# The first feed-forward's down projection as seven half-sized products

## What is computed

```python
def causal_dwconv(x, w, b):
    y = lax.conv_general_dilated(x, w[:, None, :], window_strides=(1,), padding=[(K - 1, 0)],
                                 feature_group_count=C)
    return y + b

def conv_ffn(h, w_up, conv_w, conv_b, w_down):
    a = causal_dwconv(h @ w_up, conv_w, conv_b)
    gate, val = jnp.split(a, 2, axis=-1)
    return (jax.nn.silu(gate) * val) @ w_down

x = x + conv_ffn(rms_norm(x, norm_ffn_g[l]), ffn_w_up[l], ffn_conv_w[l], ffn_conv_b[l], ffn_w_down[l])
```

## Time and profile before

| | before |
|---|---|
| median of 3 runs | 2004.89 us (2002.77 to 2004.93) |
| profiled execution, its own time | 2004.43 us |
| its span | 2002.7 us |
| TensorE busy | 1975.7 us |
| VectorE busy | 1243.9 us |
| ScalarE busy | 875.4 us |
| GpSimd busy | 109.8 us |
| first feed-forward, transposes of its norm to those of the next | 645.9 to 1010.3 us |
| second feed-forward, likewise | 1598 to 1933 us |

### The profile page before, as it was taken

One profiled execution on the slowest core, in us unless ns is written; L12 is line 12 of the kernel. 1 busy time (PEld: TensorE's weight loads), 2 busy tenths in 40 slices (PEclk: granted clock), 3 DMA queues, 4 the chain that ended last, 5 costly groups with the idle time before them and its releaser, 6 DMA issues.

```text
span 2002.7 us, 23836 instructions
## 1 busy us (share of the span) xinstructions
PE 1975.7 (99%) x9638; PEld 1629.4 (81%) x9638; DVE 1243.9 (62%) x1734; ACT 875.4 (44%) x1222; POOL 109.8 (5%) x120
## 2 busy tenths in 40 slices
PE   8999999999999999999999999999999999999998
PEld 7887788878888888888888688888888888888876
DVE  6857657577444766366468878743444476858676
ACT  5647633456323433133342634542323363544555
POOL 0004300221000000000010300000000000000000
PEclk9999999999999999999999999999999999999999
DMA  4320022222433333333342123232323335233122
GB/s 136 105 84 23 22 84 85 94 69 69 133 99 105 85 88 102 101 89 95 97 136 94 64 74 98 71 102 87 105 86 104 100 110 168 63 106 128 41 100 80
DMA packets 164444, 184.47 MB, mean 92 GB/s; under 512 B 6759, under 2 KB 125798, under 8 KB 164334
## 3 DMA queue, kind: packets, MB, share of 16 engines
q1 hardware_dynamic: 161006, 175.03, 27.4%
q10 hardware_dynamic: 2624, 5.78, 0.9%
q0 software_dynamic: 704, 2.13, 0.4%
HBM read 180.81 MB, written 2.12 MB: 91 GB/s over the span
## 4 chain that ended last, share of the span: by engine, by line
PE 93%; DVE 4%; ACT 2%; issue 1%; DMA 0%; POOL 0%; DVEq 0%; SPq 0%; ACTq 0%; POOLq 0%
PE ps L516 29%; PE ps L518 28%; PE ps L517 28%; PE ps L640 2%; PE ps L675 1%; PE ps L656 1%; PE ps L712 1%; PE ps L901 1%; ACT HH L1552 0%; DVE WL L2106 0%; DVE arena_r L2986 0%; DMA W<-in_w_in_dram 0%; DVE slots_r L2106 0%; DVE arena L2915 0%; ACT WH L1488 0%
## 5 line engine op out<-in xcount | busy, mean ns | idle before, releaser
L516 PE MATMUL ps<-HH,WH 128*128 128x512 f32 (+1 forms) x1464 | 559.3, 382 | 2.5 <-DVE HL L2234 2.5
L517 PE MATMUL ps<-HL,WH 128*128 128x512 f32 (+1 forms) x1464 | 556.3, 380 | 0.0
L2106 DVE TENSOR_TENSOR WL<-W,WH 128x2048 fp32r<-128x2048 f32 (+2 forms) x150 | 340.2, 2269 | 284.9 <-ACT WH L1488 284.2
L518 PE MATMUL ps<-HH,WL 128*128 128x512 f32 (+1 forms) x1336 | 506.6, 379 | 0.0
L1488 ACT ACTIVATE WH<-W 128x2048 fp32r<-128x2048 f32 (+2 forms) x151 | 284.2, 1884 | 190.2 <-DMA W<-in_ffn_w_down_dram 46.5
L516 PEld LDWEIGHTS ps<-HH,WH 128*128 128x128 f32 x1464 | 275.6, 188 | 56.5 <-issue 2.6
L517 PEld LDWEIGHTS ps<-HL,WH 128*128 128x128 f32 x1464 | 275.6, 188 | 51.6 <-issue 0.2
L518 PEld LDWEIGHTS ps<-HH,WL 128*128 128x128 f32 x1336 | 251.4, 188 | 47.6
L516 PE MATMUL ps<-WH,arena_r 128*128 128x512 f32 (+1 forms) x584 | 227.1, 389 | 2.3 <-DVE slots_r L2106 1.7
L518 PE MATMUL ps<-WH,arena_r 128*128 128x512 f32 (+1 forms) x584 | 226.5, 388 | 0.0
L517 PE MATMUL ps<-WL,arena_r 128*128 128x512 f32 (+1 forms) x456 | 176.7, 387 | 0.0
(11 more groups left out here) (400 smaller groups left out, 2607.2 us busy)
## 6 DMA issues: line engine op xcount, KB each, us to landing
W<-in_w_in_dram SPq DMA_DIRECT2D x50, 1024.0 KB, 5.2
W<-in_ffn_w_up_dram SPq DMA_DIRECT2D x44, 512.0 KB, 5.1
arena<-in_w_ff_dram SPq DMA_DIRECT2D x18, 1024.0 KB, 5.3
W<-in_w_gate_dram SPq DMA_DIRECT2D x16, 1024.0 KB, 4.9
W<-in_w_ff_dram SPq DMA_DIRECT2D x14, 1024.0 KB, 5.2
W<-in_ffn_w_down_dram SPq DMA_DIRECT2D x10, 1024.0 KB, 5.0
W<-in_w_out_dram SPq DMA_DIRECT2D x8, 1024.0 KB, 5.0
W<-in_w_branch_dram SPq DMA_DIRECT2D x8, 1024.0 KB, 5.1
```

Of the source, the lines that this page charges most:

```text
L516: pe.matmul(out_, st[0], mv[0], start=first, stop=False, skip_group_check=chained)
L517: pe.matmul(out_, st[0], mv[1], start=False, stop=False, skip_group_check=chained)
L518: return pe.matmul(out_, st[1], mv[0], start=False, stop=last, skip_group_check=chained)
L2106: dve.tensor_tensor(low[:, 0:n], raw[:, 0:n], plain(WH[:, j % RING, 0:n]), ALU.subtract).then_inc(slab_lo, 1)
```

## The change

The four stages become one, `ffn1`. The 11 pairs of hidden tiles are taken in chunks of 2, 3, 3 and 3. TensorE makes the up tiles of a chunk and, but for the last chunk, the first tile of the next one, then the seven products of the chunk, each of pairs x 2 x 3 matmuls. A new class `Seven` holds the semaphores and the chunk sizes. The blocks of down weights are loaded into the arena, four DMAs a chunk; the part slabs need no load of their own. t1, t3, t4 are made in the arena (t1 in b12's place, t4 in b21's), t2 in a slot of `W`. The low parts lie in `WL` or in the arena. Taps stay on VectorE. A tile's taps, gate product and forms now stand together in VectorE's queue, where they were one or two tiles apart. The first and the last line of the SP part show when the next up slabs are loaded.

```diff
+            def pe_ffn1():
+                done = 0
+                for c in range(len(F1.pairs)):
+                    for i in range(done, min(FT, 2 * F1.before(c + 1) + 1)):
...
+                        if i == 0:
+                            gemm_f_by_halves(("up", i), w, 2)
+                            ring[:] = [6, 7, 2, 3]
...
+                    down_parts(c)
+            def down_parts(c):
...
+                        elif ks[0] == 0:
+                            pe.wait_ge(F1.chain_read, 8 * c + {"P6": 0, "P3": 2, "P7": 4, "P4": 6}[name] + t + 1)
...
+                products(0, part_slab(0), range(pairs))
+                m = 1
+                if last:
+                    ws = [part_slab(1), part_slab(2)]
+                    for ks in (range(pairs - 1), range(pairs - 1, pairs)):
+                        for j in range(2):
+                            products(1 + j, ws[j], ks)
+                    m = 3
+                for m in range(m, len(PARTS)):
+                    products(m, part_slab(m), range(pairs))
```

SP's queue:

```diff
+            def down_blocks(c):
+                if c == 0:
+                    sp.wait_ge(pe_done, DONE["n2", 1, KT // 2 - 1])
+                else:
+                    sp.wait_ge(*part_end_of(F1, c - 1, "P4"))
...
+                if i == ffn1_first + 3:
+                    down_blocks(0)
+                if i - 10 in F1.first[:-1]:
+                    down_blocks(F1.first.index(i - 10) + 1)
+                if i in part_of:
+                    continue
...
-                if i >= RING:
+                if i - 7 in F1.first:
+                    sp.wait_ge(*release[i - 4])
+                elif i >= RING:
```

VectorE's queue, where `n` is the slab of up tile `i` and `p` the first part slab of the chunk:

```diff
+            def block_free(c, source):
...
+                if source == "b21":
+                    dve.wait_ge(*release[p - 1])
...
+                def sums21(c):
+                    dve.wait_ge(F1.b11_in, 16 * (c + 1))
+                    dve.wait_ge(*release[F1.first[c] - 3])
...
+                c = 0
+                for i in range(FT):
+                    n, p = slab_of[("up", i), 1], F1.first[c]
+                    last = c == len(F1.pairs) - 1
+                    if n < p - 1:
+                        split(n + 2)
+                    if n == p - 4 and c > 0:
+                        sum3(c)
+                    if n == p - 3 and c == 0:
+                        sum3(c)
+                    if n == p - 3:
+                        sums21(c)
+                    if n == p - 1 and not last:
+                        split(p + 2)
+                        sum4(c)
+                    taps(i)
+                    gated(i)
+                    if n < p - 1:
+                        forms(i)
+                    if n == p - 2:
+                        split(p + 1)
+                    if n == p - 1:
+                        if last:
+                            forms(i)
+                            split(p + 2)
+                            sum4(c)
+                        add_parts(c, 0)
+                        split(p + 3)
+                        if not last:
+                            forms(i)
+                        for m in range(1, 7 if not last else 5):
+                            add_parts(c, m)
+                            split(p + m + 3 if not last else min(p + m + 3, p + 6))
+                        c += 1
+                return add_part
```

More of the change, by code:

```diff
@@ new lines, in down_parts, with part_slab, products @@
+            def down_parts(c):
+                F1.first.append(len(slabs))
+                pairs, last = F1.pairs[c], c == len(F1.pairs) - 1
+                asked = {}
+                def part_slab(m):
+                    part_of[len(slabs)] = (c, m)
+                    return slab(pairs, 512)
+                def products(m, w, ks):
+                    name, f, group, source, t0, cols = PARTS[m]
+                    forms = F1.a_forms if f == 0 else F1.b_forms if f <= 3 else F1.c_forms
+                    for t in range(2):
+                        if ks[0] == 0 and name in ("P1", "P5", "P2"):
+                            bank((F1.tag, c, group, t), counted=False, pinned=PART_BANKS[group] + t)
+                        elif ks[0] == 0:
+                            pe.wait_ge(F1.chain_read, 8 * c + {"P6": 0, "P3": 2, "P7": 4, "P4": 6}[name] + t + 1)
+                        b = ps[PART_BANKS[group] + t]
+                        for k in ks:
+                            if t == 0:
+                                pe.wait_ge(forms, F1.before(c) + k + 1)
+                            st = [form_of(F1, F1.before(c) + k, f, 1, h)[:, t * P:(t + 1) * P] for h in ("hi", "lo")]
+                            mm = product(b[:, :], st, [x[:, k, :] for x in w],
+                                         k == 0 and name in ("P1", "P5", "P2"), k == pairs - 1, True)
+                        if ks[-1] == pairs - 1:
+                            mm.then_inc(F1.part_done, 1)
+                    if ks[-1] == pairs - 1:
+                        release[F1.first[c] + m] = part_end_of(F1, c, name)
+                products(0, part_slab(0), range(pairs))
[8 more added lines that the diff above has]
+                    products(m, part_slab(m), range(pairs))
@@ L1544, in added @@
                         taken(act, ("dn2", CHUNKS - 1, "C" if t < 2 else "A", t % 2))
+                    elif tag == "ffn1":
+                        taken(act, (F1.tag, len(F1.pairs) - 1, "C" if t < 2 else "A", t % 2))
                     else:
@@ L1578, in act_norm @@
                     square(t, n)
[L1579 to L1581 removed]
+                    if tag in ("ffn1", "ffn2") and t == 1:
+                        split(stage_slabs[stages.index(tag)] + 1)
+                split(stage_slabs[stages.index(tag)] + 2 if tag in ("ffn1", "ffn2") else slab_of[tag, 0, 1] + 2)
                 evict(1)
@@ L1867, in act_band @@
+                    if n == p - 2:
[4 more added lines that the diff above has]
+                            split(p + 3)
+                        else:
+                            split(p + 3)
+                            forms(i)
+                        for m in range(4, 9 if not last else 7):
+                            split(p + m)
+                        c += 1
             def act_band():
@@ L2281, in dve_norm @@
                 made(NT - 1)
-                split(stage_slabs[-2] + 2 if tag == "ffn2" else slab_of[tag, 0, 1] + 2)
+                split(stage_slabs[stages.index(tag)] + 2 if tag in ("ffn1", "ffn2") else slab_of[tag, 0, 1] + 2)
                 lows(1)
```

281 lines of the change are left out of this document (206 added, 75 removed).

## The result

| | before | after |
|---|---|---|
| median, both kernels on one chip | 2004.56 us (4 runs) | 2030.15 us (4 runs, 2028.98 to 2030.64) |
| ratio to before | | 1.0129, 95% interval 1.0111 to 1.0146 |
| profiled execution, own time and span | 2004.43, 2002.7 us | 2030.33, 2028.6 us |

The change makes the kernel 25.6 us slower. The forecast was 2015.6 us, with 2006 to 2021: the sign held, the size did not.

A forecast was written before the change was run, and what follows sets the result against it. TensorE, busy in 99% of the span, was taken as the bound. Matmuls saved -15.0, waits +22.9 and clock +2.8 gave +10.7 us on 2004.43, 2015.1, or 2015.6 us as median; range 2006 to 2021.

The forecast's parts named there:

- The clock: Granted clock falls behind the two longest new waits, 1.4 us each: 2.8 us; bounds none and 7.0.
- TensorE's gain: Down projection of the first feed-forward: 462 matmuls instead of 528, 66 fewer at 0.2267 us, -15.0 us.
- The waits: New TensorE waits in the stage and at its end sum to 22.9 us, bounds 16.7 and 26.
- Chunk 0: TensorE waits 2.8 us at P6 for its low part and 5.3 us at P4 for its bank.
- Chunks 1 and 2: TensorE waits 0.7 us at P6 and 2.6 us at P4 in each chunk.
- Last chunk: Behind P1, TensorE waits 6.8 us for P2's low part, which stands behind the last tile's VectorE work.
- End of stage: From transposes to the next matmul, ordered like the second feed-forward's end: 1.4 us more.
- The load itself is covered by nothing else, so no faster VectorE would take this away: Ahead of P4, the next up slab's reload, issued at P6's end, takes 5.6 us; P6's end to P4's start 10.7.
- A: Rival: the forecast's waits without a fall of the clock, +7.9 us, 2012.8 us; chance 0.23.
- B: Rival: waits as short as the second feed-forward's, 4.3 us in all, 1994 us; chance 0.08.
- C: Rival: slab reload not on the path to P4, waits 13.0 us, about 2004.3 us, no change; chance 0.07.
- D: Rival: VectorE becomes the bound, 310 of 344 us, waits rise by some 8 us, 2024 us; chance 0.05.

The follow-up runs named there:

- e7: The reordered kernel: changed kernel with old bank order, P7's adds first, earlier slab load, P2's slab later, T4 and last P2 low moved; 1998.57 us, ratio 0.9972.
- e4: Changed kernel plus 77 filler matmuls, results unread, ahead of the five long waits on TensorE; 2021.09 us.
- e1: Changed kernel with only the PSUM bank order behind the new stage put back to that of before; 2023.85 us, ratio 1.0097.
- e8: e7 with the bank order at the stage's end as in the changed kernel; 2004.63 us, ratio 1.0001.
- e2: Changed kernel with P7's adds ahead of the next up slab's low part in VectorE's queue, load unmoved; 2017.82 us.
- e3: Changed kernel with the low parts of B21 and T2 exchanging slots, so the next up slab loads one product earlier; 2019.73 us.
- e6: Changed kernel with TensorE asking for P2's slab behind P5's first two pairs in the last chunk; 2029.03 us.
- e9: e7 with the next up slab's low part again ahead of P7's adds in chunks 0 to 2; 2004.12 us.

## Why the prediction was right and wrong

Two steps failed. The clock was given two falls where five came (2.8 us, measured 7.7), and the sum ended at the stage's last transposes, which put everything that the change does behind them at nothing (measured 7.2).

**TensorE's gain, -15.0 us: held.** 66 matmuls fewer, and the reordered kernel gets 7.4 us of it in the stage.

**The waits, 22.9 us: held nearly row by row.** Chunk 0: 2.8 at P6, measured 3.0; 5.3 at P4, measured 5.3. Chunks 1 and 2: 0.7 at P6, measured 0.9 and 1.0; 2.6 at P4, measured 2.6 and 2.4. Last chunk 6.8, measured 8.0: VectorE began on the last taps 1.6 us behind the last up tile and not 0.7, and stayed one microsecond late. End of stage 1.4, measured 1.4. In sum 24.7.

**The clock, 2.8 us: the term that was too small.** "I take a fall for each" of the two longest waits at 1.4 us. The 1.4 us are the extra time of nine 384-column matmuls in the earlier trace rows, 0.34 us each from 58.57 to 61.60 us where the step from 62.02 to 62.20 is 0.18; that two of the waits and no others would bring a fall was the author's estimate. The price of a fall was right (1.5 measured), their number was not: the clock fell behind all five waits from 2.25 us up, 7.7 us. The paragraph on the clock had all five as its bound from above, at 7.0, but the range was made with "three to four falls", 5 us; with 7.0 it would have ended at 2023, still short of 2030. e4 fills the waits with matmuls, the slow steps go and the stage gets 7.8 us back: it is TensorE's standing idle that brings them on, and not the resuming by itself. Another 1.2 us of somewhat longer steps behind each hand-over was not in the sum. The forecast took comfort from the 3.6 us at the second feed-forward's end; in those TensorE still had transposes and the granted clock was 1.00 (1933 to 1937 us), and here it had nothing; whether that is the difference was not tested. (The fall of the earlier trace rows, 0.58 over 58 to 60 us, is not the only one of that trace: the clock is at 0.51 over 1997 to 2002 us as well, behind TensorE's last matmul, where it costs nothing.)

**A step that was missing: 7.2 us outside the stage.** The change also sets the order of the banks for everything behind it, and the sum ended at the stage's last transposes. e1 and e8 show the term by itself, 6.3 and 6.1 us. Against the spans the forecast was 15.2 us short (25.9 less 10.7): 7.2 here, 4.9 of clock, 1.8 of waits (the last chunk's above all) and 1.2 of hand-overs.

**"The load itself is covered by nothing else, so no faster VectorE would take this away": wrong as a cause, right as a number.** The 5.3 and twice 2.6 us came out as computed. But e2 keeps the load where it is and moves two adds, and the wait at P4 is gone; 1.8 us of it are left in chunk 0, ahead of the next up tile. The path ran through VectorE's queue order.

**The rivals.** A (no fall of the clock) is refuted for this kernel; e4 shows what it would have been, 2021 us with the bank term. B (the second feed-forward's short waits) was wrong for this change and right as a possibility: e7's waits cost 5.9 us in the stage by their steps and 1.4 at its end, under the 15.0 from which it decides. C (reload not on the path) did not happen in the changed kernel; e3, with the slab loaded earlier, comes near it in chunks 1 and 2 (0.9 us left of each wait), and e2 clears the same waits in another way, by the order of the queue. D (VectorE the bound) is refuted: with 305 busy us in 356.7 VectorE leaves TensorE busy for 351.0 us of them, at a granted clock of 1.00. That VectorE would stand near 310 us held.

**What stays open.** The waits at P6 of chunks 1 and 2 are 0.8 us in the changed kernel's trace and 1.2 to 1.8 in those of e1 and e6, which don't touch them. The traces lead from there to VectorE's delay and, in chunk 1 of e1, to a slab that came 1.5 us later; why it came later is not shown. The remaining 4.6 us of e7's waits are VectorE's backlog by their releaser; moving a tap to ScalarE, which has 205 us free in the stage, was not tried.

## What to carry over

When a change moves a matmul engine from never waiting to waiting several times, price each wait twice, in length and in slow steps behind it (here 23.3 and 7.7 us in the stage, the slow steps only behind waits of 2.25 us and more), and look for the small operation that stands behind a late large one in an in-order queue. Where a stage ends by resetting a shared rotation (banks, slots), follow that rotation to the next place where something is pinned, however far away. Compute the waits from the queues in the order they are written: that part can be right to some tenths of a microsecond.

## What the runs showed of the hardware

Falls of the granted clock behind waits of TensorE with nothing to do, from 640 to 1060 us of the ten profiled executions with the seven products; a fall is a stretch of steps of 0.43 us within 8 us behind the wait (granted clock 0.50 over 718 to 721 us of the changed kernel):

| wait (in brackets in the timeline) | waits | followed by a fall |
|---|---|---|
| 1.57 to 1.90 us | 12 | none |
| 2.25 to 2.85 us | 17 | 12 |
| 4.69 to 8.57 us | 9 | 9 |

In the middle row the length does not decide: 2.82 us (changed kernel) and 2.83 us (e2, e3) at P6 of chunk 0 were followed by a fall, 2.83 us in e1 was not; 2.25 us was in the changed kernel, 2.26 us in e3 and 2.73 us in e9 were not. Behind the long waits the slow steps begin 0.4 to 0.6 us after TensorE has resumed, behind those of the middle row 0.3 to 1.6 us (716.70 to 717.98 above). A fall cost 1.5 us in the first feed-forward of the changed kernel (7.7 us for five), and up to 2.9 us (14 slow steps) behind the longest wait of e1, 7.89 us; behind the 12 waits of 1.57 to 1.90 us no such steps stand.
